# A ring of 20 instead of 18 slots for streamed expert weights in a two-layer hybrid encoder

## What is computed

```python
def hier_moe(h, w_grp, b_grp, w_rexp, b_rexp, w_gate, w_up, w_down):
    ...
    for g in range(N_GROUPS):
        a = jnp.einsum('nd,edf->nef', x, w_gate[g])
        u = jnp.einsum('nd,edf->nef', x, w_up[g])
        hid = jax.nn.silu(a) * u * gates[:, g, :, None]
        out = out + jnp.einsum('nef,efd->nd', hid, w_down[g]).astype(F32)
```

## Time and profile before

| | us |
|---|---|
| median of 3 runs | 939.35 (938.27 to 939.6) |
| span of the profiled execution | 935.8 |
| median less span (what lies around the span) | 3.6 |
| TensorE busy in the span | 867.1 |
| expert stage of layer 0, first gate matmul to last down matmul | 255.5 to 478.9 |
| expert stage of layer 1, the same | 695.4 to 917.6 |

### The profile page before, as it was taken

One profiled execution on the slowest core, in us unless ns is written; L12 is line 12 of the kernel. 1 busy time (PEld: TensorE's weight loads), 2 busy tenths in 40 slices (PEclk: granted clock), 3 DMA queues, 4 the chain that ended last, 5 costly groups with the idle time before them and its releaser, 6 DMA issues.

```text
span 935.8 us, 14070 instructions
## 1 busy us (share of the span) xinstructions
PE 867.1 (93%) x5406; PEld 503.1 (54%) x5406; DVE 338.3 (36%) x813; ACT 213.6 (23%) x464; POOL 89.6 (10%) x106
## 2 busy tenths in 40 slices
PE   8999999999989999988768999989998999988874
PEld 6888888788733333333235555548973333333331
DVE  1522563542621111102045689973251111101105
ACT  4423233522301111101123222345121111111010
POOL 1400000000011111101000000000001111111110
PEclk9999999999999999989998999999999999999998
DMA  9962720676799999999999222035549999999995
GB/s 357 413 257 86 191 102 1 249 322 223 295 350 398 417 416 419 417 418 419 418 396 403 91 91 91 2 118 192 213 138 405 419 418 417 418 417 419 420 394 206
DMA packets 49443, 276.91 MB, mean 296 GB/s; under 512 B 11017, under 2 KB 11169, under 8 KB 20633
## 3 DMA queue, kind: packets, MB, share of 16 engines
q1 hardware_dynamic: 35472, 244.94, 64.7%
q0 software_dynamic: 13328, 30.02, 9.2%
q10 hardware_dynamic: 576, 1.05, 0.3%
HBM read 267.62 MB, written 30.61 MB: 319 GB/s over the span
## 4 chain that ended last, share of the span: by engine, by line
PE 66%; DMA 12%; SPq 11%; DVE 6%; issue 2%; ACT 2%; DVEq 0%; ACTq 0%; POOLq 0%
PE PS L1068 13%; PE PS L638 13%; SPq L410 11%; DMA slot<-in_experts 9%; PE PS L1186 9%; PE PS L1091 7%; PE PS L898 7%; PE PS L875 2%; PE PS L1045 2%; DMA XGT<-rows,IDX 2%; PE PS L1205 2%; DVE X L1551 2%; PE PS L1112 1%; PE PS L1004 1%; DVE YC L2018 1%
## 5 line engine op out<-in xcount | busy, mean ns | idle before, releaser
L1068 PE MATMUL PS<-slot,XG 128*64 128x512 f32 x1024 | 234.5, 607 | 27.8 <-DMA slot<-in_experts 26.0
L1068 PEld LDWEIGHTS PS<-slot,XG 128*64 128x64 f32 x1024 | 74.3, 139 | 163.9 <-issue 160.3
L1882 DVE SCALAR_TENSOR_TENSOR hid_by_token<-PS,SC,SG 128x256 f32<-128x256 f32 x32 | 15.5, 484 | 350.9 <-ACT SG L1447 350.9
L638 PE MATMUL PS<-slot,HT 128*128 128x256 f32 x576 | 131.4, 383 | 1.0 <-ACT HT L1287 1.0
L1091 PE MATMUL PS<-slot,HID 128*64 128x512 f32 x512 | 118.2, 604 | 5.4 <-DMA slot<-in_experts 4.3
L638 PEld LDWEIGHTS PS<-slot,HT 128*128 128x128 f32 x576 | 107.3, 190 | 19.1 <-ACT HT L1287 3.3
L1186 PE MATMUL PS<-HC,slot 128*128 128x384 f32 x256 | 86.0, 491 | 1.6 <-DVE HC L1967 1.6
L1461 ACT ACTIVATE Y<-PS,SC 128x1024 f32<-128x1024 f32 x32 | 35.7, 1114 | 159.4 <-PE PS L1091 150.8
L1091 PEld LDWEIGHTS PS<-slot,HID 128*64 128x64 f32 x512 | 36.0, 138 | 63.0 <-issue 61.6
L1186 PEld LDWEIGHTS PS<-HC,slot 128*128 128x128 f32 x256 | 47.6, 190 | 40.2 <-issue 9.7
L1447 ACT ACTIVATE SG<-PS,SC 128x256 f32<-128x256 f32 x32 | 15.2, 475 | 224.6 <-PE PS L1068 224.6
(11 more groups left out here) (305 smaller groups left out, 830.2 us busy)
## 6 DMA issues: line engine op xcount, KB each, us to landing
slot<-in_experts SPq DMA_DIRECT2D x192, 1024.0 KB, 16.5
slot<-in_w_pw SPq DMA_DIRECT2D x12, 1024.0 KB, 9.7
slot<-in_w_in SPq DMA_DIRECT2D x11, 1024.0 KB, 11.9
outs<-slot POOLq DMA_DIRECT2D x12, 512.0 KB, 10.3
slot<-outs SPq DMA_DIRECT2D x6, 1024.0 KB, 7.1
slot<-in_w_out SPq DMA_DIRECT2D x4, 1024.0 KB, 7.7
rows<-X POOLq DMA_DIRECT2D x6, 512.0 KB, 8.3
KTC<-in_k_past POOLq DMA_DIRECT2D x1, 2048.0 KB, 13.6
```

The costliest lines, as they stand in the source:

```text
L638: last = mm(PS[:, in_bank(n), 0:UCOL], HT[:, k, P * t:P * (t + 1)], w[:, k, :], start=k == 0, stop=k == KD - 1)
L1068: last = mm(PS[CAP * e:CAP * (e + 1), 2 + p % 2, :], XG[:, p % 2, k, CAP * e:CAP * (e + 1)], w[:, 2 * FE * (k % 4):2 * FE * (k % 4 + 1)], ...
```

## The change

The ring gets two more slots, 18 and 19. They lie between slots 5 and 6 and overlay nothing. Their 16 KB per partition come from the scratch of the dynamic DMAs, 2,048 bytes instead of the default 16,384, and from `VR`/`RB`, which now share `YD`'s memory. The places are no longer `q % 18`: a table `TURN` of 48 entries maps a load of either half to one of the 20 places. It reads 0 to 19, 0 to 19, and then 6 to 13. `held_before(q)` finds the load that was last in the place of q. `HOLDS` gives the slot of a place, `FREE` the order in which slots come free, and the first 20 loads of a layer are issued in that order. `NEEDED` and `freed` are unchanged. The tenth pair of slots uses the semaphore `cst_in`. Loads of layer 1 at the time when X is done are 8 instead of 6.

```diff
-LO, HI, SLOTS = 6, 12, 18
-RINGS = ((17, 6, 7, 8, 16, 9, 15, 14, 13, 12, 10, 11, 0, 1, 2, 3, 4, 5), ...
+LO, HI, SLOTS = 6, 12, 20
+HOLDS = ((0, 1, 6, 7, 8, 17, 16, 15, 14, 13, 9, 12, 10, 11, 2, 3, 4, 5, 18, 19), ...
+FREE = ((19, 18, 6, 7, 8, 17, 9, 16, 15, 14, 13, 12, 10, 11, 0, 1, 2, 3, 4, 5), ...
+FIRST = [[holds.index(n) for n in free] for holds, free in zip(HOLDS, FREE)]
...
+SHIFT = 14
+TURN = [*range(SLOTS), *range(SLOTS), *range(SLOTS - SHIFT, SLOTS - SHIFT + HALF - 2 * SLOTS)]
 def place(q):
-    return q % HALF % SLOTS
+    return TURN[q % HALF]
...
+def held_before(q):
+    return next(n for n in range(q - 1, q - HALF - 1, -1) if place(n) == place(q))
...
-        Z = slot[17][:, 0:D]
+        Z = slot[18][:, 0:D]
...
-        VR = rc("VR", [P, TOK])
-        RB = VR
+        RB = VR = YD
...
                 for q in (q for q in NEEDED if q >= SLOTS):
-                    freed(b, q - SLOTS)
+                    freed(b, held_before(q))
                     expert_load(lay, q)
...
                     for q in NEEDED:
-                        freed(b + half * (NP // 2), q - SLOTS if q >= SLOTS else q + SLOTS * (laps(q) - 1) - HALF)
+                        freed(b + half * (NP // 2), held_before(q))
                         expert_load(lay, q, half % 2)
...
+            first = iter(FIRST[0])
+            expert_load(0, next(first))
             sp.wait_ge(S("zeroed"), 16 * 4 * NT)
-            expert_load(0, 0)
+            expert_load(0, next(first))
...
                     sp.wait_ge(S("x_done"), NT)
-                    for q in range(6):
+                    for q in FIRST[1][0:8]:
                         expert_load(1, q)
...
-    nc = bacc.Bacc("TRN2", target_bir_lowering=False, num_devices=1)
+    nc = bacc.Bacc("TRN2", target_bir_lowering=False, num_devices=1, dynamic_dma_scratch_size=2048)
```

More of the change, by code:

```diff
@@ L55 @@
 UNIT = 2048
-LO, HI, SLOTS = 6, 12, 18
-RINGS = ((17, 6, 7, 8, 16, 9, 15, 14, 13, 12, 10, 11, 0, 1, 2, 3, 4, 5), (6, 7, 8, 9, 10, 11, 12, 13, 14, 15, 16, 17, 0, 1, 2, 3, 4, 5))
+LO, HI, SLOTS = 6, 12, 20
+HOLDS = ((0, 1, 6, 7, 8, 17, 16, 15, 14, 13, 9, 12, 10, 11, 2, 3, 4, 5, 18, 19), (18, 19, 6, 7, 8, 9, 10, 11, 0, 1, 12, 13, 14, 15, 16, 17, 2, 3, 4, 5))
+FREE = ((19, 18, 6, 7, 8, 17, 9, 16, 15, 14, 13, 12, 10, 11, 0, 1, 2, 3, 4, 5), (18, 19, 6, 7, 8, 9, 10, 11, 0, 1, 12, 13, 14, 15, 16, 17, 2, 3, 4, 5))
+FIRST = [[holds.index(n) for n in free] for holds, free in zip(HOLDS, FREE)]
 LOADS = 6 * NE // 2
@@ L61, with lap, loaded @@
 NEEDED += [HALF + n for n in (-6, -5, -8, -7, -4, -3, -2, -1)]
+SHIFT = 14
+TURN = [*range(SLOTS), *range(SLOTS), *range(SLOTS - SHIFT, SLOTS - SHIFT + HALF - 2 * SLOTS)]
 def place(q):
-    return q % HALF % SLOTS
+    return TURN[q % HALF]
 def laps(q):
-    return len(range(place(q), HALF, SLOTS))
+    return TURN.count(place(q))
+def lap(q):
+    return TURN[:q % HALF].count(place(q))
+def held_before(q):
+    return next(n for n in range(q - 1, q - HALF - 1, -1) if place(n) == place(q))
+def loaded(q):
+    n = place(q) // 2
+    return (f"ex_full{n}", 0) if n < 9 else ("cst_in", 16)
 UNITS = NP + 2
@@ L236, in build @@
         slot = [keep(f"slot{i}", [P, UNIT]) for i in range(LO)]
+        spare = [keep(f"slot{i}", [P, UNIT]) for i in range(18, SLOTS)]
         hi_at = keep.n
@@ L239, in build @@
         arena = keep.n
-        top_at = limit - 4 * UNIT * (SLOTS - HI)
-        slot += [nc.alloc_sbuf_tensor_at(f"slot{i}", [P, UNIT], F32, offset=top_at + 4 * UNIT * (i - HI)) for i in range(HI, SLOTS)]
+        top_at = limit - 4 * UNIT * (18 - HI)
+        slot += [nc.alloc_sbuf_tensor_at(f"slot{i}", [P, UNIT], F32, offset=top_at + 4 * UNIT * (i - HI)) for i in range(HI, 18)]
+        slot += spare
         C = {n: cst[:, x0:x1] for n, (x0, x1) in CONSTS.items()}
@@ L300, in build @@
         STN = under_c("STN", [P, 4, RH, RV])
-        assert under_c.n <= ra.n <= top_at + 4 * UNIT * 5
+        assert under_c.n <= ra.n <= limit
         RC = {n: rcst[:, x0:x1] for n, (x0, x1) in RCONSTS.items()}
@@ L408, in expert_load @@
             def expert_load(lay, q, half=0):
-                sp.dma_start(slot[RINGS[lay][place(q)]][:, :], experts[bass.ds(half * HALF + (lay * LOADS + q), 1), :, :].rearrange("o p n -> p (o n)")).then_inc(
-                    S(f"ex_full{place(q) // 2}"), 16)
+                sp.dma_start(slot[HOLDS[lay][place(q)]][:, :], experts[bass.ds(half * HALF + (lay * LOADS + q), 1), :, :].rearrange("o p n -> p (o n)")).then_inc(
+                    S(loaded(q)[0]), 16)
             def freed(b, q):
@@ L445, in _ @@
             sp.wait_ge(S("qkt_dve"), 2 * NT)
-            expert_load(0, 1)
-            expert_load(0, 2)
+            expert_load(0, next(first))
+            expert_load(0, next(first))
             sp.wait_ge(S("mixr_ready"), 1)
-            expert_load(0, 3)
-            sp.wait_ge(S("scores_masked"), FH + 2)
-            expert_load(0, 4)
+            expert_load(0, next(first))
+            sp.wait_ge(S("scores_masked"), FH + 1)
+            expert_load(0, next(first))
             sp.wait_ge(S("mr_tr"), NT)
-            expert_load(0, 5)
-            for q, heads in ((6, 4), (7, 6), (8, FH)):
+            expert_load(0, next(first))
+            for heads in (3, 5, 7, FH):
                 sp.wait_ge(S("scores_masked"), FH + heads)
-                expert_load(0, q)
+                expert_load(0, next(first))
             sp.wait_ge(S("attn_done"), ITEMS)
-            expert_load(0, 9)
+            expert_load(0, next(first))
             sp.wait_ge(S("mf_tr"), NT)
[L460 to L464, removed]
+            for _ in range(4):
+                expert_load(0, next(first))
+            for u in range(4):
+                sp.wait_ge(S("out_done"), 2 * NT - 1 + u // 2)
+                expert_load(0, next(first))
             n0 = expert_loads(0, 0)
@@ L468, in _ @@
             for i in range(12):
-                if i < 4:
-                    sp.wait_ge(S("gu_done"), b1 * 2 - 5 + i // 2)
+                if i < 2:
+                    sp.wait_ge(S("gu_done"), b1 * 2 - 8)
+                elif i < 4:
+                    sp.wait_ge(S("d_done"), b1 - 2)
                 elif i < LO:
-                    sp.wait_ge(S("d_done"), b1 - 2)
+                    sp.wait_ge(S("gu_done"), b1 * 2 - 3)
                 else:
@@ L487, in _ @@
                     sp.wait_ge(S("x_done"), NT)
-                    for q in range(6):
+                    for q in FIRST[1][0:8]:
                         expert_load(1, q)
             sp.wait_ge(S("glu_done"), KD)
-            for q in range(12, 14):
+            for q in FIRST[1][8:10]:
                 expert_load(1, q)
@@ L495, in _ @@
             sp.wait_ge(S("stored"), 16 * (STATE_STORES + CONV_STORES))
-            for q in range(6, 12):
+            for q in FIRST[1][10:16]:
                 expert_load(1, q)
-            for q in range(14, SLOTS):
-                sp.wait_ge(S("out_done"), 4 * NT - 1 + (q // 2 - 7))
+            for u, q in enumerate(FIRST[1][16:]):
+                sp.wait_ge(S("out_done"), 4 * NT - 1 + u // 2)
                 expert_load(1, q)
@@ L1050, in full_pair @@
                 def full_pair(u, q):
-                    n = laps(q)
-                    pe.wait_ge(S(f"ex_full{place(q) // 2}"),
-                               u * (32 * 2 * n) + 32 * (n * (q // HALF) + q % HALF // SLOTS + 1))
+                    n, (full_pairs, before) = laps(q), loaded(q)
+                    pe.wait_ge(S(full_pairs), before + u * (32 * 2 * n) + 32 * (n * (q // HALF) + lap(q) + 1))
                 def gate_up(b, u, p, half):
@@ L1066, in gate_up @@
                         for e in range(2):
-                            w = slot[RINGS[lay][place(6 * p + 2 * (k // 4) + e)]]
+                            w = slot[HOLDS[lay][place(6 * p + 2 * (k // 4) + e)]]
                             last = mm(PS[CAP * e:CAP * (e + 1), 2 + p % 2, :], XG[:, p % 2, k, CAP * e:CAP * (e + 1)],
@@ L1089, in down @@
                             for e in range(2):
-                                w = slot[RINGS[lay][place(6 * p + 4 + e)]][:, :].rearrange("p (j n) -> p j n", j=2)
+                                w = slot[HOLDS[lay][place(6 * p + 4 + e)]][:, :].rearrange("p (j n) -> p j n", j=2)
                                 last = mm(PS[CAP * e:CAP * (e + 1), 4 + n, :], HID[:, p % 2, j, e, :],
```

## The result

The changed kernel takes **952.64 us** (median of 4 runs, 951.22 to 954.04) against 939.48 us for the kernel before (4 runs beside it, 938.27 to 943.27): a ratio of 1.014, with a 95% interval from 1.0122 to 1.0158. It is 13.2 us slower. The forecast was 952.0, from 944 to 960. The profiled execution has a span of 950.5 us, 14.7 more than the one before.

A forecast was written before the change was run, and what follows sets the result against it. The expert weight stream, 2.68 us per load, was taken to bound both expert stages. Two fewer loads against two stops gave +5.7 and +6.9 us, span 935.8 to 948.4, plus 3.6 to the median: 952.0 us, range 944 to 960.

The forecast's parts named there:

- Part 1: Expert stages: a full ring leaves 76 loads instead of 78, ending each layer 5.4 us earlier if the stream never stopped.
- Part 2: Expert stage start: load 24 waits for `down(0)`, stopping the stream from near 266 us to 277.2, in layer 1 until 717.1.
- Part 3: Mid expert stage: load 42 waits for `down(4)` until 326.6; queue empty at 325.4, restart 0.7 us, 1.9 us per layer.
- The sum: Both expert stages: layer 0 ends 5.7 us later and layer 1 adds 6.9, together +12.6 us.
- The ring does gain: Rival for the expert stages: the deeper ring simply gains, both layers end two loads earlier, 928.6 us; chance 0.06.
- Nothing cancelled: Rival for the expert stages: stop and gain cancel because loads behind the stop run faster than 2.68 us, about 940; chance 0.04.
- TensorE was relieved: Rival at `down(0)`: TensorE is not relieved, the gather lands as late as before, 959.1 us; chance 0.10.
- The descriptor room: Rival at GpSimd's zero stores: the smaller scratch makes each wait for the one before, delaying attention by 29 us, 981; chance 0.03.
- The flow by the page: Expert load stream: at about 358 GB/s a load lasts 3.13 us, the second stop vanishes, each layer loses 6.7 us.
- What would show it: Expert stages: no loads for about 18 us after 259, gather waits gone, weight waits from about pair 7, 20 to 25 us per layer.

The follow-up runs named there:

- 18-slot control: Kernel before, still 18 slots, but places by order of issue over a cycle of 96 loads, extra-window loads behind a branch: 939.92 us, ratio 1.0000.
- ring of 18: Kernel before with 18 slots, but load 20 waits for the last use of load 4, a down weight: 961.49 us, ratio 1.0236.
- ring of 20: Changed kernel with places by order of issue over a cycle of all 96 loads of a layer, extra-window loads behind a branch: 931.19 us, ratio 0.9913.
- SHIFT = 16: Changed kernel with the table's last quarter at places 4 to 11, so load 42 takes load 26's place, a gate weight: 952.23 us, ratio 1.0136.
- small scratch: Kernel before with only the dynamic DMA scratch cut to 2,048 bytes, freed memory unused: 938.88 us, ratio 0.9996.
- cycle of 48: Changed kernel with places by order of issue, but its own 48-entry table repeated after half a layer, no branch: 939.29 us, ratio 0.9985.

## Why the prediction was right

- **Part 1, two more loads (-5.4 us a layer).** Right in kind; its size is measured between 8.0 and 10.8 us for both layers, estimated 10.7. In the profiled execution without a stop layer 0 ends 5.1 us earlier, but the medians give 8.0 us (6.2 to 10.0); the 18-slot control has nothing of it. In pairs with the stop it is 961.49 - 952.64 = 8.9 us, and the changed kernel carries its second stop in addition (0.6 + 1.3 us, see part 3), which makes 10.8.
- **Part 2, whom the third load waits for.** Right in place and time. Two loads at 259.12; `down(0)` done at 277.15, forecast 277.2; in layer 1 at 724.0, forecast 717.1 plus the 6.8 us of layer 0, 723.9. The waits of 2.93 and 2.45 us for the gather are gone from both layers, and `down(0)` takes 3.63 us. TensorE in layer 0, transposes of pair 2 and `down(0)`:

```profile
272.08 1.09 PE L1070 MATMUL PS<-cst,XGT 128*128 128x128 f32 x8
...
273.48 3.63 PE L1115 MATMUL PS<-slot,HID 128*64 128x512 f32 x16
```

- **Part 3, the second stop (1.9 us a layer).** `down(4)` ended at 326.52, forecast 326.6, but the stop was worth 0.6 us in layer 0 and 1.3 in layer 1, too little to be told in the medians of the run without it. The step that failed is the flow of the 18 loads between: the prediction let them run at full pace from 277.2. The window from 277 to 293 shows 363 GB/s; (1 - 363/418) x 16 = 2.1 us went at the first restart (1.9 in layer 1, at 368), so part of the backlog was still there when load 42's turn came. The sum has no term for the first restart and too large a one for the second. By measured terms the two cost 2.1 + 0.6 = 2.7 us in layer 0 and 1.9 + 1.3 = 3.2 in layer 1, against 1.9 in the sum. (In the rows of the second place of the change the last two, slots 16 and 15, are loads 40 and 41 and not 44 and 45. 40 loads stand ahead of load 42 all the same.)
- **The sum.** +12.6 forecast. In the traces layer 0 lost 6.75 (forecast 5.7) and layer 1 7.9 (forecast 6.9). With the measured terms for the restarts the forecasts become 6.5 and 8.2. The profiled spans differ by 14.7 us and the medians by 13.2. The profiled execution of the changed kernel took 952.28 us for a span of 950.5, and every later run also has 1.8 us around the span. The table of the kernel before has 3.6 us there, so its profiled execution took some 937.6 us, 1.8 below its median, and the 14.7 us count from there. The forecast is 0.6 us short by the medians and 2.1 us by the traces from which it was worked out; that it lies so near the median is in part luck.
- **The two halves add up.** The stop alone costs 22.3 us (ring of 18), the two slots alone bring 8.0: 14.3, against 13.2 measured together. The difference is within the intervals of the three ratios, 1.7 to 2.6 us to a side.
- **The rivals.** The ring does gain by itself, but not with this table. Nothing cancelled: the flow behind the stops was 418 and 415 GB/s, no faster than before. The two averages below 418 hold a restart each: the 415 in layer 1 after that behind `down(4)` (348 GB/s from 772 to 780), the 415 in layer 0 before the short dip at 282. TensorE was relieved (959.1 did not come). The descriptor room is ruled out.
- **The flow by the page.** The rule of the Trainium skill, "DMA: Bandwidth & Descriptors", section "Where 436 GB/s comes from", by which the HBM side binds at about 358 GB/s, does not hold for this kernel: it took 418 GB/s for 146 us after, and 418 for 130 us in the ring of 20. That section works its figure out as half of a stack's 716 GB/s, a share for each of two cores, and here one core ran; no run shows what two would get. The prediction's estimate by that rate has a slip: it keeps 7.6 loads by 281.8, a count at 418 GB/s. At 3.13 us a load the 22.6 us from 259.2 hold 7.2, and the estimate is 3.2 x 3.13 - 4.6 = 5.4 us instead of 6.7. The forecast did not use it.
- **What would show it.** TensorE's first wait for weights in layer 0 is at pair 7, as forecast: 4.36 us ahead of its second gate half at 347.14, and the waits are 22.6 and 21.1 us (20 to 25 forecast). The stretch between the stages, the convolution module in it, kept its length to 0.05 us (702.24 - 476.17 against 695.44 - 469.42).

## What to carry to other kernels

When one in-order engine issues the loads of a ring, count for each load whose slot it takes, in the order of issue, and when that slot's last reader ends; a ring whose depth is no multiple of the pattern can put a late-freed slot in front of free ones. Give places in the order in which loads are issued, over a cycle as long as the order itself; then more slots bring most of their time (8 us here for two, of an estimated 10.7), and without it the same two slots cost 13. Add to a stop what the restart of the stream costs, here some 2 us from an empty queue. Moving the loads with free slots ahead, with the places left as they are, only moved the stop.

## What the runs showed of the hardware

- **A restart has a price of its own.** With the queue empty, the first 16 us after SyncE's issue lack about 2 us of full flow (363 and 368 GB/s), nearly all of it in the first 7 us (288 and 303 GB/s). In the run with SHIFT = 16 it is 1.8 us in layer 0 (372 GB/s from 277 to 293); before, where the queue hardly ran dry, the window at 282 lost 1 us.
- **A gather beside a full queue lands later.** Issued at about the same moment (266.65 before, 266.56 after), the gather of pair 2 held TensorE up for 2.93 us in layer 0 with four pairs of loads going out beside it, and not at all with one, in either layer. Other traces with four pairs show 2.82 us (ring of 20), 2.36 (small scratch) and 2.04 (cycle of 48). With three pairs it was 1.33 us in layer 0 and 2.50 in layer 1, as much as the four before (2.45), so the count of pairs alone does not give the size.
- **The length of a wait does not tell whether the clock falls.** In the ring of 20 the transposes of pair 2 in layer 1 stood behind a wait of 2.35 us, and the 16 matmuls of `down(0)` took 4.14 us. With the small scratch alone the same wait of 2.35 us was followed by 3.63 us, and in layer 0 of that same run a wait of 2.36 us by 5.67 us. The windows over the two, first the ring of 20, then the small scratch (last three columns: granted clock, DMA share, GB/s):

```profile
712.20:716.20 4.00, 4.00 (x18) 1.14 (x18) 0.78 (x4) 0.00 (x0) 0.99 (x1) 0.88 1.01 428
```

```profile
716.70:720.30 3.60, 3.60 (x23) 1.07 (x21) 1.20 (x5) 0.00 (x0) 0.99 (x1) 1.00 1.01 426
```

  At 1.00 the clock is at its level of 2.4 GHz all the time; at 0.88 it spent part of the stretch at 1.2 GHz. So the wait's length alone does not decide which of the two comes. `down(0)` ends up to 2.0 us later for it (5.67 against 3.63), and its end frees slots. In the trace of the cycle of 48 `down(0)` of layer 1 took 5.61 us behind a wait of 2.78; that this makes some of that run's scatter is not shown.
